# The last two output tiles of a hybrid decoder step made in halves of the tokens, output transposes moved one pair later

## What is computed

```
    x = x + jnp.sum(gates * up, axis=2) @ lp['w_out']
    x = x + jax.nn.sigmoid(x @ lp['w_pg'] + lp['b_pg']) * (ple @ lp['w_ple'])
```

## Time and profile before

| | us |
|---|---|
| median of 3 runs (1145.01 to 1150.27) | 1145.12 |
| the profiled execution | 1150.2 |
| its span | 1148.4 |
| TensorE busy | 1116.1 (97%) |
| VectorE busy | 646.7 (56%) |
| ScalarE busy | 344.5 (30%) |
| GpSimd busy | 129.4 (11%) |

### The profile page before, as it was taken

How to read it: one execution, slowest core, us unless ns; L and a number is a source line. 1 busy time by engine, 2 the same in 40 slices (tenths; PEclk the granted TensorE clock), 3 DMA queues, 4 the chain that set the end, 5 groups by cost and what they waited for, 6 DMA issues and landing times.

```text
span 1148.4 us, 22009 instructions
## 1 busy us (share of the span) xinstructions
PE 1116.1 (97%) x8504; PEld 870.1 (76%) x8504; DVE 646.7 (56%) x1474; ACT 344.5 (30%) x776; POOL 129.4 (11%) x215
## 2 busy tenths in 40 slices
PE   7999999999999999999999999999999999999996
PEld 5778777777777677879977778777777777687896
DVE  4576546766656504257557673756667633252854
ACT  1233223322334153310324332233124332432023
POOL 0111412020211000000011123301102011000000
PEclk9999999999989999999999999999999999999999
DMA  8733136422413684444346332643134167634421
GB/s 259 220 110 116 55 102 211 100 73 74 113 39 90 194 266 147 144 158 131 105 153 195 94 99 63 193 134 92 48 86 130 37 165 252 203 106 155 138 84 42
DMA packets 162659, 148.51 MB, mean 129 GB/s; under 512 B 41561, under 2 KB 144863, under 8 KB 162365
## 3 DMA queue, kind: packets, MB, share of 16 engines
q1 hardware_dynamic: 157300, 136.12, 40.1%
q0 software_dynamic: 2848, 7.79, 2.1%
q10 hardware_dynamic: 2408, 3.19, 0.8%
HBM read 135.42 MB, written 11.07 MB: 128 GB/s over the span
## 4 chain that ended last, share of the span: by engine, by line
PE 86%; DVE 8%; issue 2%; DMA 2%; ACT 1%; SPq 1%; DVEq 0%; ACTq 0%
PE psum L1226 51%; PE psum L1267 10%; PE psum L1154 5%; PE psum L1456 2%; PE psum L1439 1%; PE psum L1314 1%; PE psum L1575 1%; DMA arena<-conv_in 1%; PE psum L1841 1%; PE psum L1790 1%; PE psum L1659 1%; DVE arena L2576 1%; PE psum L1820 1%; PE psum L1675 1%; PE psum L1466 1%
## 5 line engine op out<-in xcount | busy, mean ns | idle before, releaser
L1226 PE MATMUL psum<-x_b,ring 128*128 128x288 f32 x1120 | 295.5, 413 | 0.0
L1226 PE MATMUL psum<-x_a,ring 128*128 128x288 f32 x1120 | 293.7, 411 | 0.0
L1226 PEld LDWEIGHTS psum<-x_b,ring 128*128 128x128 f32 x1120 | 206.0, 191 | 59.7 <-issue 8.4
L1226 PEld LDWEIGHTS psum<-x_a,ring 128*128 128x128 f32 x1120 | 205.0, 190 | 59.1 <-issue 8.4
L1909 ACT ACTIVATE arena<-psum 128x512 f32<-128x512 f32 (+7 forms) x184 | 78.8, 448 | 177.8 <-PE psum L1154 67.9
L1226 PE MATMUL psum<-z,ring 128*128 128x288 f32 x384 | 97.6, 407 | 0.0
L1226 PEld LDWEIGHTS psum<-z,ring 128*128 128x128 f32 x384 | 71.4, 190 | 20.3 <-issue 2.3
L1909 ACT ACTIVATE arena<-arena 128x256 f32<-128x256 f32 (+9 forms) x102 | 44.5, 464 | 52.8 <-DVE arena L2624 17.4
L1154 PE MATMUL psum<-consts,arena 128*128 128x128 f32 (+2 forms) x362 | 53.7, 281 | 6.6 <-DMA arena<-in_x_prompt 5.1
L1154 PEld LDWEIGHTS psum<-consts,arena 128*128 128x128 f32 (+2 forms) x362 | 42.8, 146 | 21.4 <-issue 7.4
L1909 ACT ACTIVATE triangles<-psum 128x512 f32<-128x512 f32 (+2 forms) x48 | 24.7, 515 | 80.7 <-PE psum L1439 59.5
(11 more groups left out here) (437 smaller groups left out, 1745.6 us busy)
## 6 DMA issues: line engine op xcount, KB each, us to landing
ring<-in_w_in SPq DMA_DIRECT2D x72, 1024.0 KB, 5.4
ring<-in_w_branch SPq DMA_DIRECT2D x12, 1024.0 KB, 6.8
arena<-in_cache_k SPq DMA_DIRECT2D x32, 256.0 KB, 3.3
arena<-in_cache_v SPq DMA_DIRECT2D x32, 256.0 KB, 3.2
ring<-in_w_out SPq DMA_DIRECT2D x8, 1024.0 KB, 5.2
ring<-in_w_pg SPq DMA_DIRECT2D x8, 1024.0 KB, 5.2
arena<-in_state_dn SPq DMA_DIRECT2D x8, 512.0 KB, 8.3
out_dn_sample<-arena POOLq DMA_DIRECT2D x8, 512.0 KB, 5.0
```

The source lines that it names most:

```text
L1226: ins = mm(out[:, 0:NTOK], lhs, rhs(k), start=k == 0, stop=k == k_tiles - 1)
```

## The change

- In the last layer the transposes of a pair move: tiles 0 and 1 are transposed behind product 2 of pair 2 (not behind product 5 of pair 1), tiles 2 and 3 behind product 2 of pair 3, tiles 4 and 5 ahead of product 4 of pair 3. Their copies and stores move with them.
- x_out of tile 5 stands behind product 2 of pair 3 instead of product 5.
- Tiles 6 and 7 are made in halves of 144 tokens (`x_half`): the first half of 6 and the second half of 7 behind product 5, the first half of 7 behind product 4, the second half of 6 behind product 3.
- Tiles 6 and 7 are transposed and stored together (`y_end`). Tokens 0:128 of both go out as soon as the first halves are there: VectorE copies, SP issues. For the rest ScalarE copies tokens 128:256 and issues that store itself, VectorE copies the 32 sampled rows, and SP issues them. Six stores become three.

The core of the diff:

```diff
-Y_ENDS = {3: 0, 5: 4, 7: 7, 6: 6}
+Y_ENDS = {3: 0, 5: 4}
...
-            products(kind, q, 2, 7, 5)
-            if kind == "w_pg" and q:
+            last = (kind, q, l + 1) == ("w_pg", 3, DEPTH)
+            products(kind, q, 2)
+            if last:
+                add("x_out", 5)
+            if kind == "w_pg" and q > 1 and l + 1 == DEPTH:
+                add("y_out", 2 * q - 4)
+                add("y_out", 2 * q - 3)
+            products(kind, q, 7, 5)
+            if kind == "w_pg" and q and not last:
                 add("x_out", 2 * q - 1)
...
-    order.append(("y_out", DEPTH - 1, 7))
-    order.append(("y_out", DEPTH - 1, 6))
...
+        add("x_half", 6, 0)
+        add("x_half", 7, 1)
+        add("y_out", 4)
+        add("y_out", 5)
+        products("w_pg", 3, 4)
+        add("x_half", 7, 0)
+        products("w_pg", 3, 3)
+        add("y_end", 0)
+        add("x_half", 6, 1)
+        add("y_end", 1)
+        add("y_end", 2)
...
+            def x_half(l, m, h):
+                if h:
+                    act.wait_ge(S.sem("bank2_read"), S.count("bank2_read", pos[("w_pg", l, 3, (3, 5)[m % 2])]))
+                    gate_tanh(m, 1, TG[:, 1, m % 2, HALVES[1]], "z_tanh")
+
+            def y_end(l, i):
+                if i == 2:
+                    act.wait_ge(S.sem("edge_t"), S.count("edge_t"))
+                    fn(STG[:, 1, 1, 256:512], y_last[1][:, 0:256], ACT.Copy).then_inc(S.sem("y_rows_a"), 1)
+                    act.wait_ge(S.sem("y_rows_a"), S.count("y_rows_a"))
+                    act.dma_start(O["y_prompt"][0, 128:256, 768:1024], STG[:, 1, 1, 256:512]).then_inc(S.sem("y_stored"), 16)
...
+                link(stt(TMP[:, m % 2, n], TG[:, 1, m % 2, n], 1.0, PLO[:, m, n], ADD, MUL))
+                tt(H(l)[:, m, n], TMP[:, m % 2, n], X(l)[:, m, n], ADD).then_inc(S.sem("x_next"), 1)
```

More of the change, by code:

```diff
@@ L254 @@
     "tri_iup": {"lev": (1, lambda st: st[3] < NLEV - 1), "as_sq": (1, None), "bs_sq": (1, None)},
-    "x_next": {"x_out": (1, None)},
-    "edge_t": {"x_in": (2, None), "y_out": (1, lambda st: st[2] in Y_ENDS)},
+    "x_next": {"x_out": (1, None), "x_half": (1, None)},
+    "edge_t": {"x_in": (2, None), "y_out": (1, lambda st: st[2] in Y_ENDS), "y_end": (1, lambda st: st[2] != 1)},
     "x_t": {"x_in": (2, None)},
@@ L605, in schedule @@
                     add("p_ple", m)
-            elif kind == "w_pg" and l + 1 == DEPTH:
-                add("y_out", 2 * q - 2)
-                add("y_out", 2 * q - 1)
             behind = (kind, q)
-        products("w_pg", 3, 4, 3)
-        add("x_out", 7)
-        add("x_out", 6)
-    order.append(("y_out", DEPTH - 1, 7))
-    order.append(("y_out", DEPTH - 1, 6))
+        if l + 1 < DEPTH:
+            products("w_pg", 3, 4, 3)
+            add("x_out", 7)
+            add("x_out", 6)
+            continue
+        add("x_half", 6, 0)
[9 more added lines that the diff above has]
+        add("y_end", 2)
     return order
@@ L1855, in y_out @@
                     pe.wait_ge(S.sem("ple_read"), S.count("ple_read"))
-                if m in (4, 6):
+                if m == 4:
                     pe.wait_ge(S.sem("y_rows"), S.count("y_rows", pos[("y_out", l, m - 1)]))
```

66 lines of the change are left out of this document (53 added, 13 removed).

## The result

The changed kernel takes 1140.61 us (median of 9 runs, 1139.07 to 1143.22) where the kernel before, run beside it, takes 1145.89 us (9 runs, 1144.12 to 1150.27). The medians differ by 5.3 us. The ratio, which is that of the means, is 0.9946 with an interval of 0.9930 to 0.9961: 6.2 us less, between 4.5 and 8.0. So the kernel is faster, clear of the scatter, by about half a per cent; whether it is more or less than 0.5% these runs don't tell. The time lies in the range given; the gain had been put at 6.5 us.

What follows compares the result with a forecast made beforehand. TensorE, busy for 97% of the span, was taken as the bound, so only its idle time and the tail could be won. 4.75 + 1.77 = 6.5 us off the median of 1145.12 gave 1138.6, range 1137.4 to 1141.0.

Steps and rivals of the forecast that it cites:

- The transposes one pair later: Last layer's w_pg products: six transposes per pair run where their tiles are long done; last product 4.75 us earlier.
- C: Section from the start of product 1.5 (pair 1, product 5) to the start of 3.5; forecast 15.02 us.
- A: Section from the start of product 1.5 to the start of the last product, 3.3; forecast 17.76 us.
- B: Section from the start of the last product, 3.3, to the end of the span; forecast 6.65 us.
- The halves: Tail behind product 3.5: tiles 6 and 7 in half operations of 0.31 us; together with the stores 1.77 us.
- hand-overs cost more: Rival: tail steps passing between engines cost 1.0 to 2.5 us more, gain 4.0 to 5.5, about 1140.3; chance 0.18.
- The stores: End of the program: second queue worth 0.3 to 0.5 us; ScalarE's 128 KB store lands 1.9 us after issue.
- D: Section from the start of product 3.5 to the end of the span; forecast 9.41 us.
- The clock: Rival: the clock falls before the last transposes, costing 0.8 us at most, 1139.4; chance 0.03.
- The late landing: Rival: ScalarE's last store lands as late as 7.2 us after issue, gain 1.2; chance 0.04, of which 0.02 slower.
- TensorE's waits: Rival: idle time turns into waits for weight sums or PSUM, leaving only the second term, 1143.3; chance 0.05.
- The change doesn't do what it says: Rival: the moved transposes would still wait for their tiles; given no chance of its own.

Runs made afterwards that it cites:

- e1: Kernel before with only the transposes and tile 5's x_out moved; tiles 6 and 7 whole, six stores on SP: 1143.16 us, ratio 0.9976.
- e5: Changed kernel with tile 5's x_out back behind product 3.5: profile only, A 18.97, B 7.00 us.
- e8: Changed kernel with transposes of tiles 0 to 3 behind product 1 of pairs 2 and 3, not product 2: profile only, A 19.19, B 7.26 us.
- e4: Changed kernel with tiles 7 and 6 finished whole, transposes and stores still joint: profile only, A 17.91, B 7.99 us.
- v2: Changed kernel with own PSUM banks for tiles 4 and 5, a copy moved to ScalarE, tile 7's last transposes earlier: 1141.87 us, ratio 0.9940.
- e3: Changed kernel with ScalarE's last 128 KB store issued by SP between its two others: profile only, B 6.93 us.
- e6: Changed kernel without ScalarE's last 128 KB store, so part of the output is never written: profile only, B 6.48 us.
- e7: Changed kernel with the last two stores swapped, ScalarE issuing the 32 KB and SP the 128 KB: profile only, B 6.94 us.
- e9: Changed kernel with one long-fulfilled VectorE wait kept only ahead of tile 6's first half: profile only, B 6.97 us.
- v4: v2 with both last stores on SP, fulfilled waits left out as in e9, tile 7's first half behind product 3.3: 1139.22 us, ratio 0.9926.
- e10: Changed kernel with VectorE's copy of tiles 4 and 5 ahead of tile 7's second half: profile only, B 7.04 us.

## Why the prediction was right, and where it was not

**What bounds the kernel.** Right: only idle time of TensorE, and what follows its last work, could be won, and both were.

**The transposes one pair later (4.75 forecast, 4.60 measured).** Right in mechanism and nearly in size. Products stand 0.98 apart; six transposes without a wait cost 0.65, exactly as read from eight in a row. C is 15.03 where the working gives 15.02. e1 shows the term alone (A 4.60 less, B unmoved), e5 shows that the move of tile 5 is needed for it (1.06), e8 that one product of cover would not have been enough. The mis-sized part is the stall ahead of tile 4's transposes: 0.13 forecast, 0.27 measured. VectorE's 512-wide copy took the 0.69 of the earlier trace rows, but started 0.42 us after 3.5 where the sum had 0.29. These rows of the changed kernel show what came first:

```profile
1126.16 0.46 DVE L2591 TENSOR_TENSOR x_a<-tmp,x_b 128x288 f32<-128x288 f32 x1
1126.17 0.41 ACT L1950 ACTIVATE arena<-arena,params_half 128x144 f32<-128x144 f32 x1
...
1126.76 0.46 DVE L2590 SCALAR_TENSOR_TENSOR tmp<-arena 128x288 f32<-128x288 f32 x1
```

Tile 5's x_out, which the change moved forward, starts 0.14 us after the end of tile 4's, 0.18 after ScalarE's tanh is done at 1126.58. The sum let it follow without a gap.

**The halves (part of 1.77 forecast, 1.42 measured).** Half operations took 0.31, as priced from the 144-wide read. e4 puts the halves at 1.0. Of the tail, compare each step by its distance from the start of 3.5:

| step | forecast | changed kernel |
|---|---|---|
| read of 3.5 done | 1.69 | 1.66 |
| tile 6, first half done | 2.3 | 2.22 |
| tile 7, second half done | 2.9 | 3.20 |
| tile 7, first half done | 4.06 | 4.35 |
| tile 6, second half done | 5.76 | 6.05 |
| last ScalarE copy done | 6.88 | 7.18 |
| SP's last issue | 7.0 | 7.32 |
| end of the span | 9.41 | 9.88 |

One step is late, by 0.3, and all behind it carry it on: tile 7's second half, because of the gap that no row of before showed. The step of the prediction that is off is the sentence that puts "0.02 to 0.03 between" half operations everywhere. The rival "hand-overs cost more" had this sort of loss, at 1.0 to 2.5 us; it was 0.3. But the gap is only one half of it. The sum also let tile 7's first half start 3.41 us after 3.5, with the tanh of product 3.4 done at 3.31, and had nothing for the way from ScalarE to VectorE (only the rival "hand-overs cost more" had), although a row of the kernel before shows it:

```profile
1141.81 0.46 DVE L2537 SCALAR_TENSOR_TENSOR tmp<-arena 128x288 f32<-128x288 f32 x1 [0.18 <-ACT arena L1909]
```

The gap and the stall hide each other: in v2, where neither the copy nor the stall stands in the way, tile 7's first half starts 1.77 us after product 3.4 and waits for its tanh. With the stall, 3.4 starts 1.90 after 3.5, so without the gap that half could not have started before 3.67 where it started at 3.70; and e8 took the stall away, and the end stayed. e5 is near to the missing test: it has no gap, and its tile 7's first half still comes no earlier, 1.76 us after product 3.4, with the tanh as what ended the wait, and B is 7.00:

```profile
1131.78 0.31 DVE L2602 SCALAR_TENSOR_TENSOR tmp<-arena 128x144 f32<-128x144 f32 x1 [0.37 <-ACT arena L1948]
```

So taking away the gap alone, or the stall alone, gives nothing back; by these rows it takes both. (The 3.67 is worked out; no run had the stall without the gap and was otherwise the same, for in e5 tile 5's x_out moves too.)

The Trainium skill (VectorE: DVE Perf Modes, The TRN2 errata) gave 58 cycles plus one per element, 0.21 us for 144, as a rival to the row's 0.31. The trace agrees with the row: every half operation is 0.30 or 0.31. The same section has for fp32 tensor_tensor (N + 151) / 0.96 ns; that gives 0.307 for 144 and 0.457 for 288 as estimates from that page. The traces agree: 0.31 and 0.46 for the tensor_tensor rows. Its advice against small tiles weighs a fixed cost per instruction; here the halves pay that cost, and e4 shows that they still win 1.0 us, by what no longer queues behind a whole tile.

**The stores.** This step failed twice. The second queue was priced as a gain of 0.3 to 0.5 us; e3 shows that it is worth nothing (B 6.93 on one queue, 7.00 on two). And the store that ends the program was not the one that was priced: ScalarE's 128 KB landed in 1.9 as forecast, SP's 32 KB, issued 0.11 us later, in 2.1. e6 and e7 show that it is the large store beside it, and neither queue, that costs: alone the 32 KB take 1.5. This is the other 0.17 of the 0.47 us that D is over its forecast, and by one profile each it is at the edge of what D can show. The sentence on the Trainium skill (DMA: Bandwidth & Descriptors, Issuing engines are not separate DMA queues) stood there as the other side, and its result is the one that came: nearly nothing. The reason differs from the rule's, though. The issue time saved is not small here (0.26 us); it is lost again because the small store lands behind the 128 KB one in any case, and that one is not issued any earlier.

**The rivals.** The clock did not fall ahead of the last transposes: the window over the end shows it, and the four transposes took 0.66. The late landing did not come (1.9). TensorE's waits did not move elsewhere: up to the last product the only one left in pairs 2 and 3 is the 0.24 ahead of tile 4's transposes. Of the signs named for a right forecast one did not come: from the last product to the end it is 7.0 us, not 6.6. "The change doesn't do what it says" was given no chance, rightly.

**The time itself.** 1138.6 was forecast and 1140.61 measured. Of these 2.0 us, 0.8 is the kernel before, 1145.89 in its 9 runs where 1145.12 was the median at hand; 0.5 is the tail; the 0.7 left can't be told from the scatter of single runs (4 us within the 9). By the time alone, the rival "hand-overs cost more" with its 1140.3 would fit better than the 1138.6. What decides for the forecast is the 6.02 us by the sections, inside its 5.7 to 7.3 and short of the 6.5 by 0.5, where the rival had at least 1.0.

## What to carry to other kernels

Take the transposes, copies and stores of finished tiles off the place where the tile has just been made, and put them a stage later: the cost of a group then falls from what it waits for to what it issues (2.41 to 0.65 us here), as long as the wait that was removed is fully covered; one product too few, and 0.77 us of each group are back. At the end of a program, ask which engine's queue everything passes through, and count from the last point where that queue was free (product 3.5 here, not the last product). Do not count on a second queue for the last small stores without measuring the landing: here the small store landed just behind the large one from either queue, so that nothing was won. For a change of a few us in a kernel of a thousand, compare starts within a profile, from a mark just ahead of the change.

## What the runs showed of the hardware

**Half clock far from the change.** Product 1.5, which nothing in these kernels moves, starts between 1109.20 and 1117.47. Five of the fourteen profiles (before, e1, e4, e9, v2) have a stretch of half clock between 320 and 335 us; their product 1.5 starts at 1116.12 to 1117.47, that of the nine others at 1109.20 to 1113.05. The window in before and in the changed kernel (columns as in the earlier trace rows, the granted clock is the third number from the end):

```profile
320.00:335.00 15.00, 12.79 (x249) 9.69 (x249) 7.12 (x18) 4.60 (x6) 1.58 (x3) 0.77 0.17 65
```

```profile
320.00:335.00 15.00, 12.72 (x258) 10.30 (x259) 9.24 (x26) 4.03 (x7) 1.41 (x2) 1.00 0.07 24
```

0.77 over 15 us is about 6.9 us at 1.2 GHz where the rest ran at 2.4. The program is the same in all fourteen up to the last layer's w_pg, and no part of the change goes with it: e1 has it and e3 hasn't. The earlier trace rows were read from it. Half clock for 6.9 us is 3.4 us of work done late: most, but not all, of the 4.9 us of TensorE's busy time and of the 5.2 by which product 1.5 is later in before, and so one reason why the spans of before and after differ by 11.2 us where the stretch of the change gives 6.02. What sets it off is open.

**Two stores that end together.** A 32 KB store landed in 1.5 us alone (e6), in 1.7 when issued 0.4 us behind a 128 KB one on the same queue (e3, v4), and in 2.0 to 2.1 when issued 0.1 us behind it from another queue (changed kernel, e7), whichever queue had which. The 128 KB took 1.9 each time, and the 32 KB landed 0.2 to 0.3 after them.

**A gap without a cause.** 0.31 to 0.34 us of VectorE behind tile 6's first half, in all nine kernels where that half follows the read of 3.5 at once (changed kernel, e3, e6, e7, e8, e9, e10, v2, v4), and none where an x_out stands between (e5). It did not depend on the next instruction (e10), on the one fulfilled wait that e9 takes away, or on transfers (e8). A half that follows a read at once does not always have it: in v4 tile 7's first half follows the read of 3.3, and the next starts 0.03 us behind it.
